# Latent queries' rotation: the identity product is dropped, and VectorE adds the turned rows to the part held in memory

## The chip, the cores and the metric

The kernel runs on one core of one Trainium2 chip. The metric is the device time of one execution in microseconds, from the first instruction to the last; lower is better. In each view PE is TensorE's matmuls, PEld its weight loads, DVE is VectorE, ACT is ScalarE, POOL is GpSimd.

## The reference, cut to what matters

The program is two models one after the other: a first block (dilated attention, a linear recurrence, two feed-forward parts) and then a second block of two equal layers. Each layer of the second block has three kinds of attention, one of them the "latent" one, which the change touches. It has 4 heads, 64 plain and 32 rotated dimensions per head, and a sequence of 512:

```
q = (rms_norm(c_q) @ w_uq)              # 512 x 4 heads x 96
k = concat(k_nope, k_r)                 # 64 own rows, 32 rows common to the heads
q = rms_norm(q, q_g);  k = rms_norm(k, k_g)
q = concat(q[:64], rope(q[64:], pos))   # the same for k
rope(x): concat(x1*cos - x2*sin, x2*cos + x1*sin)
p = softmax(mask(q @ k.T * 96**-0.5));  o = p @ v
```

So a rotated query is the query times a table of cosines, plus the query with its two halves exchanged (one with its sign turned) times a table of sines. Everything else in the program is unchanged and is left out here.

## The kernel before, in words

Activations lie transposed: features in the 128 partitions, the 512 tokens in the free dimension. Float32 products are made of three products of a high and a low part (`three`, L753 to L759). The high part is written by ScalarE, the low part by VectorE. Every engine has a program of its own, and they meet only at semaphores; the order on each engine is the order in which it is written.

Of a layer of the second block, the latent attention is the part named `mla_...`. A head (index h) goes through these steps:

- `mla_products(h)` on PE makes the head's raw query (96 rows) and raw key (64 rows) in two PSUM banks. Two banks are all that this part has for such outputs, so every use waits until VectorE has counted the bank of two uses ago as read (`acc_freed`).
- ScalarE squares both (`mla_squares`, L2244). VectorE's `mla_evict` writes the gained query times the cosine table to `turned` (L3130, a slice of the tile `sd`; in the 64 plain rows the table holds ones), the gained query times the sine table to `vt2` (L3132), and the gained key to `tn` (L3136).
- PE's `mla_sums` (L1396 to L1410) sums the key's squares over the rows (L1400) and then fills a second bank with the rotated query: an identity product that brings in `turned` (L1407) and a product with the constant `TURN`, which exchanges the halves of the 32 rotated rows of `vt2` and has zeros elsewhere (L1408). These are float32 products of 96x96 by 96x512, and the trace has two records for each.
- ScalarE's `mla_hi` makes the key's factor (L2254, L2258). VectorE's `mla_lo` multiplies the key by it (L3142) and then the rotated query in PSUM by its own factor `rs` (L3145). ScalarE copies both as high parts (L2261, L2267), VectorE writes both low parts (L2889).
- PE's `mla_scores(h)` (L1421 to L1424) makes four blocks of scores in four "wide" banks, with the sum for the next head's query factor (L1166) in front of the fourth. VectorE takes four maxima (L3168), ScalarE four exponentials (L2291), VectorE a reciprocal (L3176) and four scalings (L3180).
- PE's `mla_turn` transposes the weights into the wide banks (L785, L787), ScalarE copies them (L2058), VectorE takes the low parts (L2914) and so frees the wide banks for the next head's scores. `mla_weigh` applies them to the values.

The loop over the heads is written out. For head h, PE's order is: products of h+1, scores of h, weighing of h-1, sums of h+1, turning of h. VectorE's order is: `mla_evict` of h+1, maxima, output of h-1, reciprocal and scalings, `mla_lo` of h+1, low parts of the turned weights. So VectorE's `mla_lo` of the next head stands between the scalings of this head and the low parts that free the wide banks. Head 0's `mla_sums` and `mla_lo` stand ahead of the loop; behind `mla_lo(0)` ScalarE squares an output (L2023), PE sums the squares (L1166), ScalarE makes a factor of the sum (L2031), and PE turns a tile of values (L785, L787) in the same bank. Ahead of that sum PE runs ten matmuls whose result nobody reads (`unread_wide`, L778).

`mla_sums` runs 8 times in all: four heads in each of two layers.

Of the kernel before, what the change touches and what calls it, by code (L numbers as in the profile page):

```python
# [22 lines left out]
ALU = mybir.AluOpType  # L23
# [4 lines left out]
S = 512  # L28
# [30 lines left out]
MLA_W = 96  # L59
# [178 lines left out]
IDENT, ONES, HALVES, TURN, LATER, MINUS, FORBID = range(7)  # L238
# [27 lines left out]
def build_program(nc, t, out):  # L266

    with ExitStack() as ctx:
# [12 lines left out]
        sems = {n: ctx.enter_context(nc.semaphore(n)) for n in names}  # L281

        def sb(name, shape, dt=F32, c=ctx):
            return c.enter_context(nc.sbuf_tensor("s_" + name, shape, dt))

        bank = [ctx.enter_context(nc.psum_tensor(f"acc{n}", [P, S], F32)) for n in range(3)]
# [14 lines left out]
        square = sb("square", [P, FORBID + 1, P])  # L301
# [108 lines left out]
        tn = sb("tn", [P, 2, S], F32, stage)  # L410
        rs = sb("rs", [P, S], F32, stage)
# [11 lines left out]
        vt2, kr = (sb(n, [P, S], F32, sub) for n in ("vt2", "kr"))  # L423
        sd = sb("sd", [P, 2, TRI[TT]], F32, sub)
# [310 lines left out]
        def _(pe):  # L735
            count = Counts(pe)
            mm = nc.tensor.matmul
# [61 lines left out]
            for n, (a, b) in enumerate([(0, S), (S, 2 * S), (2 * S, F_W)]):  # L799
                o = wide[n // 2][0:GROUPS * HEADS, (n % 2) * S:(n % 2) * S + b - a]  # L800
# [319 lines left out]
            def layer(i):  # L1120
# [273 lines left out]
                def mla_sums():  # L1394


                    pe.wait_ge(sems["mla_sq"], count("mla_sq"))
                    if past := count("acc_freed", lag=count.banks):
                        pe.wait_ge(sems["acc_freed"], past)
                    mm(bank[count.bank()][0:MLA_W, :], square[0:MLA_W, ONES, 0:MLA_W], sq[0:MLA_W, 1, :], start=True,  # L1400
                       stop=True).then_inc(sems["acc_full"], 1)
                    count("acc_full")
                    count.outs += 1
                    if past := count("acc_freed", lag=count.banks):
                        pe.wait_ge(sems["acc_freed"], past)
                    o = bank[count.bank()][0:MLA_W, :]
                    mm(o, square[0:MLA_W, IDENT, 0:MLA_W], sd[0:MLA_W, 1, 0:S], start=True, stop=False)  # L1407
                    mm(o, square[0:MLA_W, TURN, 0:MLA_W], vt2[0:MLA_W, :], start=False, stop=True).then_inc(sems["acc_full"], 1)  # L1408
                    count("acc_full")
                    count.outs += 1  # L1410

# [36 lines left out]
                mla_values()  # L1448
                query_sum()
                mla_sums()  # L1450
                count("hn_lo")
                unread_wide(10, ckh)
# [3 lines left out]
                for h in range(HEADS_2):  # L1456
                    if h < HEADS_2 - 1:
                        mla_products(h + 1)
                    mla_scores(h)
                    if h == HEADS_2 - 1:  # L1460
                        head_sum(HALVES)
                    if h:
                        mla_weigh(h - 1, TT)
                    if h < HEADS_2 - 1:
                        mla_sums()
                    mla_turn()
# [86 lines left out]
                def mem_bank():  # L1553
                    if past := count("acc_freed", lag=count.banks):
                        pe.wait_ge(sems["acc_freed"], past)
                    o = bank[count.bank()]
                    count.outs += 1
                    return o
# [10 lines left out]
                for u in range(2):  # L1569
                    if u:  # L1570
                        pe.wait_ge(sems["unit_ready"], count("unit_ready"))
                    for n in range(0 if u else 2, 4):
                        o = mem_bank()
# [844 lines left out]
        def _(dve):  # L2418
            count = Counts(dve)
            count.squares = 0  # L2420
            tt, stt, ts = nc.vector.tensor_tensor, nc.vector.scalar_tensor_tensor, nc.vector.tensor_scalar

            def output():
                dve.wait_ge(sems["acc_full"], count("acc_full"))
                o = acc[count.bank()]
                count.outs += 1
                return o
# [447 lines left out]
            def layer(i):  # L2875
# [11 lines left out]
                def head_lo(dst, src, hi, scale=1.0):  # L2887
                    dve.wait_ge(sems["hn_hi"], count("hn_hi"))
                    stt(dst, src, scale, hi.bitcast(F32), ALU.mult, ALU.subtract).then_inc(sems["hn_lo"], 1)  # L2889
                    dve.wait_ge(sems["hn_lo"], count("hn_lo"))  # L2890
# [231 lines left out]
                R, KR = slice(0, MLA_W), slice(SUB, MLA_W)  # L3122
                turned, rs_k = sd[:, 1, 0:S], sd[:, 1, S:2 * S]
# [15 lines left out]
                def mla_lo(h):  # L3139
                    dve.wait_ge(sems["hn_rstd"], count("hn_rstd", 2))  # L3140
                    output()
                    tt(kr[R, :], tn[R, 1, :], rs_k[R, :], ALU.mult).then_inc(sems["acc_freed"], 1)  # L3142
                    dve.wait_ge(sems["acc_freed"], count("acc_freed"))
                    o = output()
                    tt(tn[R, 0, :], o[R, :], rs[R, :], ALU.mult).then_inc(sems["acc_freed"], 1)  # L3145
                    dve.wait_ge(sems["acc_freed"], count("acc_freed"))
                    head_lo(mla_k[h % 2][1], kr[R, :], mla_k[h % 2][0])
                    head_lo(mla_q[h % 2][1], tn[R, 0, :], mla_q[h % 2][0], MLA_W ** -0.5)
# [10 lines left out]
                mla_evict()  # L3159
                mla_values()  # L3160
                mla_lo(0)
                head_norm([(yo[:, 5, :], od[:], 0)], "sb_out_g_2")
                memory_values_lo()
                for h in range(HEADS_2):
                    if h < HEADS_2 - 1:
                        mla_evict()
                    for q in range(TT):
                        nc.vector.tensor_reduce(sm[:, q:q + 1], next_wide()[:, 0:(q + 1) * P], AX_X, ALU.max,  # L3168
                                                negate=True).then_inc(sems["nmax_ready"], 1)
                        count("nmax_ready")  # L3170
                    if h == HEADS_2 - 1:
                        mla_norm(0)
                    if h:
                        take_output(slice(SUB * ((h - 1) % 2), SUB * ((h - 1) % 2 + 1)))
                    dve.wait_ge(sems["exp_done"], count("exp_done", TT))
                    nc.vector.reciprocal(sm[:, 16:20], sm[:, 8:12]).then_inc(sems["recip"], 1)  # L3176
                    dve.wait_ge(sems["recip"], count("recip"))
                    for q in range(TT):
                        w = slice(TRI[q], TRI[q + 1])
                        ts(sd[:, 0, w], sd[:, 0, w], sm[:, 16 + q:17 + q], None, ALU.mult).then_inc(sems["wide_freed"], 1)  # L3180
                        count("wide_freed")
                    if h < HEADS_2 - 1:
                        mla_lo(h + 1)
                    else:
                        ys(range(3))
                    for q in range(TT):
                        turned_a(q)
# [60 lines left out]
                for n in range(2):  # L3248
                    o = output()
# [87 lines left out]
```

## Time and profile before

| | us |
|---|---|
| median of 3 runs | 3185.25 |
| lowest and highest | 3183.9, 3186.6 |
| the profiled execution's own time | 3184.36 |
| its span in the trace | 3182.5 |
| mean granted clock of TensorE | 0.988 of full |

A row of a timeline gives the start, the duration, the engine, the line, the operation with its tiles, and in square brackets how long the engine had been idle and what released it. Where a row says "x2", two records stand in it. Weight loads have rows of their own (PEld). Time in which an engine waited for nothing that the profile shows is called "issue".

### The profile page before, as it was taken

What the parts mean: (1) busy time and instruction counts of PE and PEld (TensorE: products, weight loads), DVE (VectorE), ACT (ScalarE), POOL (GpSimd) and SP (SyncE); (2) the same over time, 40 slices, a digit from 0 to 9 for tenths busy, and PEclk for the clock granted to TensorE, in tenths of its full rate; (3) what the DMA queues carried; (4) which work ended last, traced back from release to release, by engine and by line L of the source; (5) the groups of instructions that cost most, each with busy time, mean ns of one, the idle gap of its engine ahead of it and who ended that gap; (6) DMA issues with size and microseconds to landing.
All of it is one profiled execution on the core that took longest, in us unless ns stands there. A gap on an engine that the chain in (4) does not pass through costs nothing.

```text
span 3182.5 us, 44000 instructions
## 1 busy us (share of the span) xinstructions
PE 3071.7 (97%) x13735; PEld 2433.7 (76%) x13735; DVE 1632.5 (51%) x2425; ACT 1444.4 (45%) x2116; POOL 737.1 (23%) x508
## 2 busy tenths in 40 slices
PE   8999999999999999999999889999999988999998
PEld 6888888788887777888867667788887775778887
DVE  6544455585565878575668464511125746441113
ACT  4333334453334775342356764522245666552224
POOL 2333323100000000000022213244443220334444
PEclk9999999999999999999999999999999999999999
DMA  5333322333332232433312112133332210223334
GB/s 159 106 98 87 93 75 78 90 117 102 97 92 86 67 106 80 139 94 93 86 54 61 58 37 67 47 97 95 92 119 67 60 56 27 67 70 96 93 92 132
DMA packets 490394, 273.00 MB, mean 86 GB/s; under 512 B 9550, under 2 KB 479766, under 8 KB 489848
## 3 DMA queue, kind: packets, MB, share of 16 engines
q1 hardware_dynamic: 485576, 264.45, 28.9%
q10 hardware_dynamic: 4656, 6.58, 0.6%
q8 instruction: 78, 1.28, 0.2%
q14 instruction: 84, 0.69, 0.1%
HBM read 267.69 MB, written 12.21 MB: 88 GB/s over the span
## 4 chain that ended last, share of the span: by engine, by line
issue 56%; PE 30%; POOL 11%; DVE 2%; ACT 1%; POOLq 0%; ACTq 0%; DMA 0%; DVEq 0%
PE acc L753 9%; PE acc L754 9%; PE acc L759 8%; POOL s_w_lo L722 5%; POOL s_w_lo L721 5%; PE acc L756 1%; PE wide L785 1%; PE misc L754 0%; PE misc L753 0%; PE misc L759 0%; DVE s_sc L2610 0%; PE wide L753 0%; POOLq L111 0%; PE wide L754 0%; PE misc L785 0%
## 5 line engine op out<-in xcount | busy, mean ns | idle before, releaser
L753 PE MATMUL acc<-s_h_hi,s_w_hi 128*128 128x512 f32 (+1 forms) x1920 | 787.6, 410 | 15.0 <-DVE s_h_lo L3049 8.3
L754 PE MATMUL acc<-s_h_lo,s_w_hi 128*128 128x512 f32 (+1 forms) x1920 | 754.0, 393 | 0.0
L721 POOL TENSOR_TENSOR s_w_lo<-s_raw,s_w_hi 128x512 fp32r<-128x512 f32 x212 | 275.7, 1300 | 2035.3 <-ACT s_w_hi L1622 2034.0
L759 PE MATMUL acc<-s_h_hi,s_w_lo 128*128 128x512 f32 (+1 forms) x1680 | 660.5, 393 | 0.0
L1622 ACT ACTIVATE s_w_hi<-s_raw 128x1024 fp32r<-128x1024 f32 x386 | 409.6, 1061 | 367.6 <-DVE s_x L3298 211.3
L753 PEld LDWEIGHTS acc<-s_h_hi,s_w_hi 128*128 128x128 f32 x1920 | 363.8, 189 | 113.1 <-issue 16.9
L754 PEld LDWEIGHTS acc<-s_h_lo,s_w_hi 128*128 128x128 f32 x1920 | 364.5, 190 | 86.4 <-issue 11.3
L759 PEld LDWEIGHTS acc<-s_h_hi,s_w_lo 128*128 128x128 f32 x1680 | 318.6, 190 | 73.3
L704 POOL TENSOR_TENSOR s_w_lo<-s_raw,s_w_hi 128x1024 fp32r<-128x1024 f32 x80 | 191.6, 2395 | 403.3 <-ACT s_w_hi L1622 401.7
L722 POOL TENSOR_TENSOR s_w_lo<-s_raw,s_w_hi 128x512 fp32r<-128x512 f32 x212 | 278.6, 1314 | 0.0
L753 PE MATMUL acc<-s_hid_hi,s_w_hi 128*128 128x512 f32 x704 | 278.1, 395 | 0.0
L754 PE MATMUL acc<-s_hid_lo,s_w_hi 128*128 128x512 f32 x704 | 277.9, 395 | 0.0
L759 PE MATMUL acc<-s_hid_hi,s_w_lo 128*128 128x512 f32 x616 | 243.2, 395 | 0.0
L3288 DVE SCALAR_TENSOR_TENSOR s_u<-acc,s_rstd 128x512 f32<-128x512 f32 x64 | 44.3, 692 | 267.6 <-PE acc L756 260.1
L753 PE MATMUL wide<-s_h_hi,s_w_hi_f 128*128 128x512 f32 x384 | 153.4, 399 | 3.2 <-DVE s_h_lo L2444 3.2
L754 PEld LDWEIGHTS acc<-s_hid_lo,s_w_hi 128*128 128x128 f32 x704 | 132.4, 188 | 31.4
L753 PEld LDWEIGHTS acc<-s_hid_hi,s_w_hi 128*128 128x128 f32 x704 | 132.4, 188 | 31.4
L1840 ACT ACTIVATE s_cv<-s_up,s_cols 128x512 f32<-128x512 f32 x96 | 78.6, 819 | 162.0 <-DVE s_up L2690 157.7
L754 PE MATMUL wide<-s_h_lo,s_w_hi_f 128*128 128x512 f32 x384 | 151.7, 395 | 0.0
L2698 DVE SCALAR_TENSOR_TENSOR s_cv<-s_up,s_cols,s_cv 128x512 f32<-128x512 f32 x192 | 144.1, 750 | 6.1
L3298 DVE TENSOR_TENSOR s_x<-s_x,acc 128x512 f32<-128x512 f32 x48 | 33.0, 688 | 222.0 <-PE acc L756 222.0
L759 PEld LDWEIGHTS acc<-s_hid_hi,s_w_lo 128*128 128x128 f32 x616 | 115.9, 188 | 27.7
(498 smaller groups left out, 5414.9 us busy)
## 6 DMA issues: line engine op xcount, KB each, us to landing
s_raw<-w_ff SPq DMA_DIRECT2D x128, 512.0 KB, 4.0
s_raw<-ffn_w_up SPq DMA_DIRECT2D x96, 512.0 KB, 3.9
s_raw<-attn_w_qkv SPq DMA_DIRECT2D x72, 512.0 KB, 3.8
s_raw<-ffn_w_down SPq DMA_DIRECT2D x48, 512.0 KB, 3.9
s_raw<-w_in SPq DMA_DIRECT2D x48, 512.0 KB, 4.0
s_raw<-lru_w_in SPq DMA_DIRECT2D x16, 512.0 KB, 3.9
s_raw<-w_out SPq DMA_DIRECT2D x16, 512.0 KB, 4.0
s_bd<-bias_by_head SPq DMA_DIRECT2D x24, 256.0 KB, 5.0
```

Source lines behind the costliest of these rows:

```text
L704: pool.tensor_tensor(w_lo_of[w][:], raw[s][:], w_hi_of[w][:].bitcast(F32), ALU.subtract).then_inc(sems["unit_ready"], 1)
L721: pool.tensor_tensor(w_lo_b[s][:, 0:h, :], raw_b[s][:, 0:h, :], w_hi_b[s][:, 0:h, :].bitcast(F32), ALU.subtract)
L722: pool.tensor_tensor(w_lo_b[s][:, h:, :], raw_b[s][:, h:, :], w_hi_b[s][:, h:, :].bitcast(F32), ALU.subtract).then_inc(sems["unit_ready"], 1)
L753: mm(out, ahi, bhi, start=start, stop=False, **kw)
L754: mm(out, ahi, blo, start=False, stop=False, **kw)
L756: mm(out, alo, bhi, start=False, stop=stop, **kw).then_inc(sems[sem], 1)
L759: mm(out, alo, bhi, start=False, stop=stop, **kw)
L1622: fn(dst[:], src[:], ACT.Copy).then_inc(sems["hi_split"], 1)
L1840: fn(cv[:, s, :], up[:, s, 2:2 + S], ACT.Identity, bias=cols[:, bass.ds(b * KC + v, 1)], scale=cols[:, bass.ds(b * KC + w, 1)]).then_inc(s ...
L2698: stt(cv[:, s, :], up[:, s, tap:tap + S], cols[:, bass.ds(b * KC + w, 1)], cv[:, s, :], ALU.mult, ALU.add).then_inc(sems[sem], 1)
L3288: stt(u2[:, n % 2, :], o[:], 0.0, rstd[:], ALU.max, ALU.mult).then_inc(sems["acc_freed"], 1)
L3298: tt(x[:, n, :], x[:, n, :], o[:], ALU.add).then_inc(sems["acc_freed"], 1)
```

## The change

`mla_sums` no longer makes the identity product. The product with `TURN` starts and ends its bank's sum by itself, and the bank then holds only the turned rows. In `mla_lo` VectorE first adds the 32 rotated rows of that bank (`KR`, partitions 64 to 95) onto `turned` in place, waits for its own result, and multiplies `turned` instead of the bank by `rs`. The bank is counted as read by the multiplication, as before.

```diff
@@ mla_sums, TensorE
-                    o = bank[count.bank()][0:MLA_W, :]
-                    mm(o, square[0:MLA_W, IDENT, 0:MLA_W], sd[0:MLA_W, 1, 0:S], start=True, stop=False)
-                    mm(o, square[0:MLA_W, TURN, 0:MLA_W], vt2[0:MLA_W, :], start=False, stop=True).then_inc(sems["acc_full"], 1)
+                    mm(bank[count.bank()][0:MLA_W, :], square[0:MLA_W, TURN, 0:MLA_W], vt2[0:MLA_W, :], start=True,
+                       stop=True).then_inc(sems["acc_full"], 1)
@@ mla_lo, VectorE
                     o = output()
-                    tt(tn[R, 0, :], o[R, :], rs[R, :], ALU.mult).then_inc(sems["acc_freed"], 1)
+                    tt(turned[KR, :], o[KR, :], turned[KR, :], ALU.add).then_inc(sems["a_mid"], 1)
+                    dve.wait_ge(sems["a_mid"], count("a_mid"))
+                    tt(tn[R, 0, :], turned[R, :], rs[R, :], ALU.mult).then_inc(sems["acc_freed"], 1)
                     dve.wait_ge(sems["acc_freed"], count("acc_freed"))
```

## Rows read from the trace of the kernel before

**Rows 1.** Page, part 1: busy us (share of the span) and instructions.
```profile
PE 3071.7 (97%) x13735; PEld 2433.7 (76%) x13735; DVE 1632.5 (51%) x2425; ACT 1444.4 (45%) x2116; POOL 737.1 (23%) x508
```

**Rows 2.** Timeline of the first layer, PE's sums for heads 0 and 1.
```profile
1858.12 1.10 PE L1407 MATMUL acc<-s_sd,s_square 96*96 96x512 f32 x2
...
1871.98 1.02 PE L1407 MATMUL acc<-s_sd,s_square 96*96 96x512 f32 x2
...
1872.83 1.02 PE L1408 MATMUL acc<-s_vt,s_square 96*96 96x512 f32 x2
```

**Rows 3.** The line of the identity product, both layers.
```profile
L1407 PE MATMUL acc<-s_sd,s_square x16: 592/592/670, 1858.1 to 2677.6; 96*96 96x512 f32 x16
```

**Rows 4.** Timeline of the first layer, around head 0's query and what follows it.
```profile
1859.85 0.69 DVE L3142 TENSOR_TENSOR s_kr<-s_tn,s_sd 96x512 f32<-96x512 f32 x1
...
1860.66 0.69 DVE L3145 TENSOR_TENSOR s_tn<-acc,s_rs 96x512 f32<-96x512 f32 x1
1861.38 0.63 ACT L2267 ACTIVATE s_h_hi<-s_tn 96x512 fp32r<-96x512 f32 x1 [0.18 <-DVE s_tn L3145]
...
1862.12 0.63 ACT L2023 ACTIVATE s_sq<-s_od 128x512 f32<-128x512 f32 x1
...
1862.88 1.12 PE L1166 MATMUL misc<-s_sq,s_square 128*128 128x512 f32 x2 [0.51 <-ACT s_sq L2023]
...
1864.86 0.55 PE L785 MATMUL misc<-s_square,s_cq 128*128 128x128 f32 x3 [0.86 <-ACT s_rs L2031]
```

**Rows 5.** The lines of two other VectorE operations on 32 partitions, both layers.
```profile
L3090 DVE TENSOR_TENSOR s_cq<-misc,s_rope x2: 689/689/689, 1832.7 to 2611.6; 32x512 f32<-32x512 f32 x2
...
L3094 DVE TENSOR_TENSOR s_tn<-s_tn,s_cq x2: 1661/1662/1664, 1834.1 to 2613.3; 32x512 f32<-32x512 f32 x2
```

**Rows 6.** Timeline of the first layer, from head 0's scalings to head 1's scores.
```profile
1874.77 0.18 DVE L3176 RECIPROCAL s_sm<-s_sm 128x4 f32<-128x4 f32 x1 [2.75 <-ACT s_sd L2291]
...
1875.32 0.33 PE L787 MATMUL wide<-s_square,s_sd 128*128 128x128 f32 x1 [1.47 <-DVE s_sd L3180]
...
1879.66 1.74 DVE L2914 TENSOR_TENSOR s_al<-wide,s_ah 128x128 fp32r<-128x128 f32 x4 [0.21 <-DVE s_h_lo L2889]
...
1880.36 0.22 PE L1421 MATMUL wide<-s_h_hi 96*128 96x128 f32 x1
```

**Rows 7.** Timeline of the first layer, the same places for heads 2 and 3.
```profile
1888.23 0.14 PEld L787 LDWEIGHTS wide<-s_square,s_sd 128*128 128x128 f32 x1 [0.42 <-DVE s_sd L3180]
...
1892.57 0.62 DVE L2914 TENSOR_TENSOR s_al<-wide,s_ah 128x128 fp32r<-128x128 f32 x2 [0.21 <-DVE s_h_lo L2889]
...
1892.92 0.33 PE L1421 MATMUL wide<-s_h_hi 96*128 96x128 f32 x1 [0.62 <-DVE s_al L2914]
...
1905.58 0.33 PE L1421 MATMUL wide<-s_h_hi 96*128 96x128 f32 x1 [3.04 <-DVE s_al L2914]
```

**Rows 8.** PE's waits over the whole span: us in total, times, longest us.
```profile
PE wide L1421 <- DVE s_al L2914: 7.3, 4, 3.0
...
PE wide L787 <- DVE s_sd L3180: 5.7, 4, 1.5
```

**Rows 9.** Windows of 2 us, first layer: length, busy (x) of PE, PEld, DVE, ACT, POOL, PEclk, DMA.
```profile
1862.00:1864.00 2.00, 1.49 (x4) 0.30 (x2) 0.85 (x2) 0.64 (x2) 0.00 (x0) 1.00 0.00 0
1864.00:1866.00 2.00, 1.14 (x8) 0.99 (x8) 0.50 (x1) 1.74 (x3) 0.00 (x0) 1.00 0.00 0
...
1872.00:1874.00 2.00, 1.85 (x5) 0.47 (x3) 0.01 (x1) 1.67 (x7) 0.00 (x0) 1.00 0.00 0
1874.00:1876.00 2.00, 0.68 (x4) 0.43 (x5) 1.20 (x5) 1.86 (x4) 0.00 (x0) 0.96 0.01 4
1876.00:1878.00 2.00, 2.00 (x10) 1.85 (x10) 1.68 (x4) 0.98 (x3) 0.00 (x0) 0.50 0.00 0
1878.00:1880.00 2.00, 2.00 (x8) 1.29 (x7) 1.66 (x4) 1.63 (x4) 0.00 (x0) 0.69 0.00 0
```

**Rows 10.** Timeline of POOL: its first instruction after the last at 1854.90.
```profile
1931.80 1.29 POOL L721 TENSOR_TENSOR s_w_lo<-s_raw,s_w_hi 128x512 fp32r<-128x512 f32 x1 [75.61 <-ACT s_w_hi L1622]
```

## The prediction

> **What bounds the kernel now.** I read the page's first part first: PE is busy 97% of the span and VectorE 51% [rows 1]. A change that takes work from PE and gives it to VectorE looks like a gain by that. But the share is a mean over the program, and the change touches only the latent attention of two layers, some 70 us each (in the first layer from 1858 [rows 2] to 1932 [rows 10]). So I read the timeline of that stretch next, and then PE's waits. PE does not set the pace there: it waits for the low parts of the turned weights before a head's scores, 7.3 us in four waits, and for the scaled weights before their transposes, 5.7 us in four waits [rows 8]. The first layer alone shows 0.62 and 3.04 us before the scores of heads 2 and 3 [rows 7], so 3.66 of the 7.3, and the second layer repeats it. The reader is to see a ring of dependences there: scores, maxima, exponentials, reciprocal, scalings, the next head's key and query on VectorE, low parts of the turned weights, next scores. Each step waits for the one before, on another engine or on VectorE itself.
>
> **What is removed: the identity product.** Its two records start at 1871.98 and the TURN product starts at 1872.83, so it holds PE for 0.85 us [rows 2]. There are 16 records, that is 8 products [rows 3]: 6.8 us of PE's time. What is it worth? In head 1's sums PE is done with both products at about 1873.85 (1872.83 + 1.02, [rows 2]) and then idles 1.47 us until the first scaled weights are there at 1875.32 [rows 6]; ending 0.85 earlier makes that idle time 2.32 and moves nothing. For heads 2 and 3 the gap on PE is nearly closed: the weight load shows 0.42 us [rows 7]. There the transposes can start up to a few tenths earlier, but what follows waits for the low parts from VectorE (0.62 and 3.04 us, [rows 7]), so this too is worth nothing. For head 0, PE waits 0.51 us for the squares behind the query [rows 4], and again the earlier end only lengthens the wait. VectorE's multiplication does not wait for the product either: in each of the eight instances L3145 starts 0.81 us after L3142, back to back (1859.85 and 1860.66, [rows 4]). Value of the removal: nothing, as long as PE is not the last. I bound it by 0 and 6.8 us and take 0.
>
> **What is added: one VectorE addition and a wait for it.** No row has this instruction. The nearest are the product of a 32x512 PSUM operand with a 32x512 tile, 0.689 us, and an addition of two 32x512 tiles in memory, 1.66 us [rows 5]. The duration on 96 partitions is the same as on 32, 0.69 us [rows 4], so the smaller number of rows buys nothing. The 1.66 us were taken while POOL worked; here POOL does nothing for 75.6 us ahead of 1931.8, that is from 1856.2 [rows 10]. I take 0.69 us, and with the wait for its own semaphore the spacing of two dependent VectorE instructions, 0.81 us [rows 4]. Behind the addition in VectorE's queue stand the multiplication, both low parts, and the low parts of the turned weights; ScalarE's copy of the query (L2267) waits for it, and PE's next scores wait for all of these. The multiplication reads memory in place of PSUM: L3142 does that, and takes the same 0.69 as L3145 [rows 4]; cost 0.
>
> The Trainium skill, "SBUF — State Buffer", section "Who interferes with whom", says that a VectorE instruction with two SBUF inputs contends with a GpSimd instruction that reads SBUF, and that the second to issue blocks until the first is done. The new multiplication has become such an instruction. By that rule each would cost up to about a microsecond more if POOL worked beside it; POOL is idle through the stretch, so the rule leaves the sum as it is.
>
> **The delay, instance by instance.**
> - Head 0: the query is 0.81 later, ScalarE's copy and squares follow it back to back (1861.38, 1862.12), PE's sum waits for them (0.51 us idle before), then ScalarE's factor, then PE's transposes (0.86 us idle) [rows 4], then the next products and scores on PE. No slack: 0.81.
> - Head 1: the low parts that free the banks start at 1879.66, and the scores of head 1 start at 1880.36 behind PE's own products [rows 6]. At head 2 the scores start 0.35 after the first low part (1892.57 and 1892.92, [rows 7]), so head 1's scores could have started at 1880.01: slack 0.35, delay 0.81 - 0.35 = about 0.45.
> - Heads 2 and 3: PE waits for the low parts directly [rows 7]: 0.81 each.
>
> That is 0.81 + 0.45 + 0.81 + 0.81 = 2.88 us in a layer, 5.8 us in two. Nothing after it gives this back: the next products need the outputs of this attention, and weights are already waiting (POOL had stopped because its buffers were full, [rows 10]).
>
> **TensorE's clock.** More idle time can also cost clock. In the first layer the granted clock stays at 1.00 through the two windows with 1.49 and 1.14 us of PE work around head 0's sum, and it falls to 0.50 (1.2 of 2.4 GHz) after the two windows with 1.85 and 0.68 us; it is back within the window from 1878 [rows 9]. The low stretch is (0.04 x 2 + 0.50 x 2 + 0.31 x 2) / 0.5 = 3.4 us long, and costs PE half of that, 1.7 us. Before, it fell on the products of head 2, which nobody was in need of: only the slack of 0.35 above was used by it. Now take head 0's place: the unread matmuls end 0.85 earlier, the sum starts 0.81 later, so the wait before it is 0.51 + 0.85 + 0.81 = 2.2 us, with 0.86 after it [rows 4]. Of the 2.63 us of work in the two windows some 0.8 move out, leaving 1.8, less than the 2.53 after which the clock fell [rows 9]. So I expect it to fall here too. What comes next is transposes, products and scores on PE with everyone waiting, so the stretch is on the path: 1.7 us a layer at most, and 1.5 taken, since the transposes at its head are spaced by more than the clock. For two layers 3.0 us.
>
> The Trainium skill, "TensorE: Matmul & The Clock Gate", section "HAM oscillation — how this bites in real kernels", states it as a mechanism: idle gaps between bursts of matmuls put the clock back to half, and the next burst starts cold. The rule speaks against this change, which turns PE work into PE idle time, and the row of the low stretch bears it out; without the rule and the fall the sum would end at 5.8 us.
>
> **The sum.** 5.8 + 3.0 = 8.8 us. On the profiled execution's own 3184.36 (a span of 3182.5) that is 3193.2. Its time lies 0.9 below the median of the runs, 3185.25, so for a median I give 3194.1.
>
> **The rivals.**
> - Delay alone (A2): the clock does not fall at head 0, or in one layer only. 5.8 us give 3191.1, with one fall 3192.6. For it: the clock stood before with waits of 0.51 and 0.86 us. Against: the wait is now 2.2.
> - More clock is lost (A3): the wait before head 2's scores grows from 0.62 to 1.4 us, and the low stretch at head 3 grows or begins earlier; one more fall of 1.7 in each layer gives 3194.1 + 3.4 = 3197.5. Against: before 1892.9 PE has worked nearly without pause.
> - PE is the last after all (B), the other side: the 0.85 us of PE counts in each head, and the addition is hidden beside it. 3185.25 - 6.8 = 3178.4. It would need PE's sums to end later than the scaled weights are ready. Heads 2 and 3 are nearly at that point (0.42 us on the weight load, [rows 7]). It decides if the waits before L1421 are shorter than they seem; the 3.66 us a layer speak against it.
> - The delay is absorbed (C): some of it falls into slack that I don't see, as at head 1, so that less than 5 us remain: 3185.25 to 3190.
> - VectorE is slowed by POOL (D): the addition and the multiplication take 1.66 each, 8 x 2 x 0.97 = 15.5 us more: 3209.6. POOL would have to work in the stretch, and it doesn't [rows 10].
>
> **How the numbers follow.** Forecast 0.45; A2 0.30; A3 0.13; B 0.04; C 0.07; D 0.01. The range reaches from the low end of A2 (5.8 less 1 for a partly hidden instance, 3190.0) to A3's full price, 3198.0, and leaves out B, C, D and the edges of the others. 0.2% is 6.4 us, about what a measurement of this kernel can tell from no change; that is 3191.6. Slower by over that: the forecast, A3, D, and the part of A2 with one fall, 0.13, together 0.72. Within: the rest of A2 and C, 0.24. Faster: B, 0.04.
>
> **What would show it.** In the profile after, PE's busy time is lower and the kernel slower. The addition is a row of 0.69 us with the multiplication 0.81 after it; the wait before head 0's L1166 is about 2.2, before L787 of head 0 about 2.3, before L1421 about 1.4 for head 2 and 3.9 for head 3, and head 1 has a wait of some tenths where it had none. PEclk falls to 0.50 right after head 0's sum. Wrong would be: no growth of the waits before L1421 (B or C), an addition clearly longer or shorter than 0.69, or a clock that stays at 1.00 in head 0's place (then A2).

## The result, and the profile after

The changed kernel takes 3198.54 us (median of 6 runs, 3195.97 to 3201.09), the kernel before 3186.26 us beside it (6 runs, 3183.9 to 3187.34). The ratio is 1.0040, with a 95% interval of 1.0029 to 1.0051: 12.3 us slower, where 8.8 were forecast. The direction came as forecast, and so did the delay and the fall of the clock at head 0; two further costs of the clock did not, and the time lies 0.5 us above the range.

The page of the profile after, its first lines (the span is that of one profiled execution, whose own time is 3199.52):

```profile
span 3197.7 us, 43984 instructions
...
PE 3075.1 (96%) x13719; PEld 2435.8 (76%) x13719; DVE 1637.7 (51%) x2433; ACT 1443.1 (45%) x2116; POOL 736.6 (23%) x508
```

PE has 16 records fewer and VectorE 8 instructions more, which is the change. But PE's busy time is 3.4 us longer than in [rows 1], not 6.8 us shorter: the matmuls that are left took longer, which is a first sign of the clock. This is the timeline of the first layer after, the places of [rows 4, 6, 7] (start, length, engine and line, and in brackets the idle time before and what ended it):

```profile
1862.96 0.69 DVE L3141 TENSOR_TENSOR s_kr<-s_tn,s_sd 96x512 f32<-96x512 f32 x1
1863.77 0.69 DVE L3144 TENSOR_TENSOR s_sd<-acc,s_sd 32x512 f32<-32x512 f32 x1
1864.49 0.69 DVE L3146 TENSOR_TENSOR s_tn<-s_sd,s_rs 96x512 f32<-96x512 f32 x1
1865.21 0.63 ACT L2266 ACTIVATE s_h_hi<-s_tn 96x512 fp32r<-96x512 f32 x1 [0.90 <-DVE s_tn L3146]
...
1866.71 1.12 PE L1166 MATMUL misc<-s_sq,s_square 128*128 128x512 f32 x2 [2.08 <-ACT s_sq L2022]
...
1880.70 0.33 PE L787 MATMUL wide<-s_square,s_sd 128*128 128x128 f32 x1 [2.32 <-DVE s_sd L3181]
...
1899.50 0.33 PE L1420 MATMUL wide<-s_h_hi 96*128 96x128 f32 x1 [1.22 <-DVE s_al L2913]
...
1913.01 0.48 PE L1420 MATMUL wide<-s_h_hi 96*128 96x128 f32 x1 [3.76 <-DVE s_al L2913]
```

The addition (L3144) takes 0.69 us and starts 0.81 after the key's multiplication, but the query's multiplication follows it by 0.72, not 0.81. So the query comes 0.72 later. The waits are close to those that were named: 2.08 us before head 0's sum (2.2 named), 2.32 before the transposes behind head 0's scores (2.3), 1.22 before head 2's scores (1.4), 3.76 before head 3's (3.9). The wait of some tenths at head 1 did not come. In the last row the matmul itself takes 0.48 us, where [rows 7] has 0.33: it runs at a lower clock. In the waits over the whole span, these two lines answer to [rows 8] (us in total, times, longest):

```profile
PE wide L787 <- DVE s_sd L3181: 10.4, 8, 2.3
PE wide L1420 <- DVE s_al L2913: 10.0, 4, 3.8
```

The windows around head 0's sum, of after (length, busy (x) of PE, PEld, DVE, ACT, POOL, granted clock, DMA share, GB/s), where the first two of [rows 9] show 1.00:

```profile
1867.00:1869.00 2.00, 1.15 (x4) 0.32 (x4) 0.00 (x0) 1.02 (x2) 0.00 (x0) 0.91 0.00 0
1869.00:1871.00 2.00, 2.00 (x8) 1.56 (x7) 1.28 (x2) 0.90 (x2) 0.00 (x0) 0.50 0.00 0
```

The clock falls to its lower level (1.2 GHz) right behind head 0's sum, as forecast, and PE is fully busy while it is low, so this stretch is paid for.

**Where the 12.3 us are.** I cut both traces at the same instructions: the sine product of head 0 (L3132, after L3131), its key product, the first score matmul of each head, head 3's reciprocal, the first addition to the stream x. Each cell is the time from one to the next:

| us | key product | scores 0 | scores 1 | scores 2 | scores 3 | reciprocal 3 | addition to x | stage |
|---|---|---|---|---|---|---|---|---|
| before, layer 1 | 3.60 | 7.59 | 12.92 | 12.56 | 12.66 | 9.83 | 16.85 | 76.01 |
| after, layer 1 | 3.58 | 9.86 | 13.29 | 13.39 | 13.51 | 10.51 | 16.85 | 80.99 |
| before, layer 2 | 3.59 | 7.60 | 13.04 | 12.57 | 12.68 | 9.81 | 16.87 | 76.16 |
| after, layer 2 | 3.59 | 9.89 | 13.30 | 13.37 | 13.50 | 10.44 | 16.85 | 80.94 |

The stages cost 4.98 and 4.78 us more, together 9.8. The stretch from layer 1's addition to x to layer 2's sine product, in which no line was changed, is 2.3 us longer. It goes by the start times of these pairs; before:

```profile
1932.26 1.38 DVE L3197 TENSOR_TENSOR s_x<-s_x,acc 128x512 f32<-128x512 f32 x2 [1.05 <-PE acc L756]
...
2633.91 0.75 DVE L3132 SCALAR_TENSOR_TENSOR s_vt<-acc,s_cols,s_rope 96x512 f32<-96x512 f32 x1
```

after:

```profile
1940.37 0.69 DVE L3198 TENSOR_TENSOR s_x<-s_x,acc 128x512 f32<-128x512 f32 x1 [1.05 <-PE acc L756]
...
2644.34 0.75 DVE L3131 SCALAR_TENSOR_TENSOR s_vt<-acc,s_cols,s_rope 96x512 f32<-96x512 f32 x1
```

That is 701.65 before and 703.97 after. Behind layer 2's stage the two traces are equal (472.47 and 472.46 to the end). The three parts make 9.8 + 2.3 + 0 = 12.1 of the 12.3 measured. The two profiled executions differ by more, 15.2 us. The other 3.1 lie ahead of layer 1's stage, where nothing was changed: after is 3.9 us behind at 150 us, and 3.1 at the stage. At 150 us the other ten traces lie between 0.5 us ahead of before and 3.2 behind it, whatever their edit, so I take this for scatter between executions and leave it out.

### The profile page after: what moved, and what is told of

Read it like the earlier page. It is cut to its first block, busy times and chain, and to the rows that moved or that the text cites. A ratio compares the mean times of both kernels' runs of the same rounds, so it can differ in the third digit from the quotient of the medians.

```text
span 3197.7 us, 43984 instructions
## 1 busy us (share of the span) xinstructions
PE 3075.1 (96%) x13719; PEld 2435.8 (76%) x13719; DVE 1637.7 (51%) x2433; ACT 1443.1 (45%) x2116; POOL 736.6 (23%) x508
## 4 chain that ended last, share of the span: by engine, by line
issue 56%; PE 30%; POOL 11%; DVE 2%; ACT 1%; POOLq 0%; ACTq 0%; DMA 0%; DVEq 0%
PE acc L753 9%; PE acc L754 9%; PE acc L759 8%; POOL s_w_lo L722 5%; POOL s_w_lo L721 5%; PE acc L756 1%; PE wide L785 1%; PE misc L754 0%; PE misc L753 0%; PE misc L759 0%; DVE s_sc L2609 0%; PE wide L753 0%; POOLq L111 0%; PE wide L754 0%; ACTq L1668 0%
```

## The experiments

In each, "stage" and "stretch" are those of the table above. Times are medians, with the ratio to the kernel before run beside them.

**The changed kernel again**, with the first three experiments, so that they can be compared on one chip.

> The changed kernel once more, for a second trace and more timed runs. The latent stage (from head 0's key sum L1400 to the last ys product that waits) grew by 4.98 us in the first layer and 4.78 in the second in the first trace, 9.8 in all, of a difference of 15.2 between the two profiled executions. Theory A (only the stage pays, the rest is where TensorE's clock happens to fall in each execution): this trace shows 9 to 11 us again in the two stages, about 3197 us in all, and another amount outside them. Theory B (the change also costs something outside the stage, about 2.5 to 5 us): the first 1800 us are again 3.8 us longer and the stretch between the two latent stages again 2.3 us longer than in the trace of before.

3196.61 against 3185.16 us, ratio 1.0034 (1.0022 to 1.0047). The trace repeats the first to a few hundredths: stages 81.01 and 80.97, stretch 704.03. The falls of the clock are at the same places of the program in both layers, so they are no accident of one execution. The cost outside the stages is there again too (704.03 - 701.65 = 2.4 us), as the second theory had it.

**The removal alone.** The identity product and the addition both go, so this kernel leaves out the cosine part of every latent query; the query's factor is applied to the PSUM bank, as before:

```diff
-tt(turned[KR, :], o[KR, :], turned[KR, :], ALU.add).then_inc(sems["a_mid"], 1)
-dve.wait_ge(sems["a_mid"], count("a_mid"))
-tt(tn[R, 0, :], turned[R, :], rs[R, :], ALU.mult).then_inc(sems["acc_freed"], 1)
+tt(tn[R, 0, :], o[R, :], rs[R, :], ALU.mult).then_inc(sems["acc_freed"], 1)
```

> Half the change: the identity product is dropped and VectorE multiplies the bank as before, with no addition. It leaves out the cosine part of every latent query. Theory A (PE is not the last in this stage, so the product's 0.85 us are worth nothing, and more idle time can only cost clock): no faster than before, 3186.3, with the wait before head 0's sum 1.36 us in place of 0.51; if the clock falls there, up to 1.5 us a layer more, 3189.3. Rival B (PE's time is on the path, 8 x 0.85): 3179.5.

3186.79 against 3185.16 us, ratio 1.0003 (0.9994 to 1.0012). The stage of layer 1 is 76.01, that of before to the hundredth; that of layer 2 is 76.94, and what it has more comes in one step, from head 3's scores to its reciprocal (10.60 against 9.81), where its clock is low already when the scores begin. The product of 0.85 us, eight times, is worth nothing that can be measured.

**The addition alone.** The identity product is put back into its bank ahead of TURN, which overwrites it; VectorE keeps the addition:

```diff
-mm(bank[count.bank()][0:MLA_W, :], square[0:MLA_W, TURN, 0:MLA_W], vt2[0:MLA_W, :], start=True,
-   stop=True).then_inc(sems["acc_full"], 1)
+o = bank[count.bank()][0:MLA_W, :]
+mm(o, square[0:MLA_W, IDENT, 0:MLA_W], sd[0:MLA_W, 1, 0:S], start=True, stop=True)
+mm(o, square[0:MLA_W, TURN, 0:MLA_W], vt2[0:MLA_W, :], start=True, stop=True).then_inc(sems["acc_full"], 1)
```

> The other half: the changed kernel, with the identity product put back ahead of the TURN product in the same bank, where the latter overwrites it. PE has the work of before, VectorE the addition. Theory A (delay of 0.72 a head without slack, 0.4 at head 1): 2 x (3 x 0.72 + 0.4) = 5.1 us, 3191.4, if the clock stays at head 0 (wait of 0.51 + 0.72 = 1.2 us there), and 3194.4 if it falls. Rival: the whole of the change's cost comes from the addition and none from the work taken from PE: 3198.5.

3197.0 against 3185.16 us, ratio 1.0034 (1.0021 to 1.0048); stages 80.95 and 80.99, stretch 703.98. The whole cost of the change is the addition's. The two runs also test my reason for the fall of the clock at head 0: that too little of PE's work is left in the two windows of [rows 9]. Here are the wait before head 0's sum, the same two windows (from 5.75 us behind the start of the sine product) and the one behind them, first of the removal alone:

```profile
1864.72 1.12 PE L1166 MATMUL misc<-s_sq,s_square 128*128 128x512 f32 x2 [1.35 <-ACT s_sq L2022]
...
1863.86:1865.86 2.00, 1.12 (x2) 0.30 (x2) 0.83 (x2) 0.63 (x1) 0.00 (x0) 1.00 0.00 0
1865.86:1867.86 2.00, 1.16 (x7) 0.99 (x8) 0.52 (x1) 1.76 (x3) 0.00 (x0) 1.00 0.00 0
1867.86:1869.86 2.00, 2.00 (x13) 1.49 (x12) 1.37 (x3) 1.12 (x3) 0.00 (x0) 1.00 0.00 0
```

and of the addition alone:

```profile
1865.80 1.12 PE L1166 MATMUL misc<-s_sq,s_square 128*128 128x512 f32 x2 [1.20 <-ACT s_sq L2023]
...
1864.21:1866.21 2.00, 0.81 (x3) 0.30 (x2) 1.43 (x3) 1.26 (x2) 0.00 (x0) 1.00 0.00 0
1866.21:1868.21 2.00, 1.14 (x4) 0.44 (x3) 0.00 (x0) 1.14 (x2) 0.00 (x0) 0.85 0.00 0
1868.21:1870.21 2.00, 2.00 (x8) 1.55 (x7) 1.40 (x2) 0.77 (x2) 0.00 (x0) 0.50 0.00 0
```

The length of the one wait does not decide: with the longer wait, 1.35 us, the clock stands, and with the shorter, 1.20, it falls. PE's work in the two windows orders the kernels rightly. It is 2.63 us before and 2.28 in the removal alone, where the clock stands, and 1.95 in the addition alone and 1.56 after, where it falls. The removal takes its product away mostly ahead of these windows, while the delay of 0.72 us moves work out of them. But my yardstick, less than the 2.53 us at the other place, fails: 2.28 is less than that too, and the clock stands.

**More unread matmuls ahead of head 0's sum**, to keep PE at work and the clock up there. The kernel already has 10 that write a bank nobody reads:

```diff
-                unread_wide(10, ckh)
+                unread_wide(17, ckh)
```

> The changed kernel with 17 unread matmuls in place of 10 ahead of head 0's sum (7 x 0.23 = 1.6 us more of PE work in the wait of 2.1 us). Theory A (the clock that falls right after head 0's sum costs about 1.55 us a layer): the granted clock stays at full there and the kernel is 3.1 us faster than the changed one, 3195.4. Rival (the growth at head 0 from key product to scores, 2.27 us, is all delay, no clock): no difference, 3198.5.

3198.11 against 3185.16 us, ratio 1.0038 (1.0025 to 1.0052). The edit did what it was meant to do at its own place. Head 0's sum and the same windows:

```profile
1866.29 1.12 PE L1166 MATMUL misc<-s_sq,s_square 128*128 128x512 f32 x2 [0.52 <-ACT s_sq L2022]
...
1867.00:1869.00 2.00, 1.14 (x6) 0.67 (x6) 0.09 (x1) 1.33 (x3) 0.00 (x0) 1.00 0.00 0
1869.00:1871.00 2.00, 2.00 (x11) 1.38 (x10) 1.37 (x3) 1.18 (x2) 0.00 (x0) 1.00 0.00 0
```

The wait is 0.52 (0.51 in [rows 4]), PE's work in the two windows of [rows 9] is 2.62 us again, the clock stands, and from key product to scores it is 8.32 and 8.29 us instead of 9.86 and 9.89. That prices the fall at head 0 at 1.54 and 1.60 us a layer, 3.1 in all, and leaves the bare delay: 8.32 - 7.59 = 0.73, and 0.69. But the stage is 83.07 in layer 1 and 81.81 in layer 2, not shorter than after's: from head 2's scores to head 3's it now takes 15.93 and 15.90 us, where after takes 13.51 and 13.50. Windows from head 2's scores on:

```profile
1897.00:1899.00 2.00, 1.48 (x11) 1.41 (x12) 1.55 (x4) 1.68 (x3) 0.00 (x0) 0.99 0.02 4
1899.00:1901.00 2.00, 2.00 (x7) 1.47 (x6) 1.74 (x4) 0.59 (x1) 0.00 (x0) 0.50 0.00 0
1901.00:1903.00 2.00, 2.00 (x6) 1.21 (x4) 1.72 (x4) 0.71 (x2) 0.00 (x0) 0.50 0.00 0
...
1905.00:1907.00 2.00, 2.00 (x12) 1.73 (x11) 0.32 (x1) 1.41 (x4) 0.00 (x0) 0.81 0.00 0
```

A low stretch of some 6.8 us (three windows at 0.50, two of them shown, and 0.38 of the next) begins at head 2's scores, where after's clock stands at 1.00. One fall is gone and another, longer one has come. So the time is what the rival expected (3198.5, no difference), but the fall at head 0 did cost what the first theory said; it was paid elsewhere. In layer 1 head 3 costs more as well (11.02 from scores to reciprocal against 10.51, then 17.54 against 16.85), but the stretch behind is 701.40 again: the 2.3 us of after are not there. The two stages are 12.7 over before's with a stretch that costs nothing, and that comes to about as much as after's 9.8 + 2.3, by chance as far as these runs show.

**Two additions**: one more of the same kind, into a tile that nobody reads after it, ahead of the real one:

```diff
+tt(vt2[KR, :], o[KR, :], turned[KR, :], ALU.add).then_inc(sems["a_mid"], 1)
+dve.wait_ge(sems["a_mid"], count("a_mid"))
 tt(turned[KR, :], o[KR, :], turned[KR, :], ALU.add).then_inc(sems["a_mid"], 1)
```

> The changed kernel with a second addition of the same size in front of the first; its result goes to a slice that nobody reads before it is overwritten, and the addition waits for it. Theory A (the steps between the key product and the next scores are one chain with no slack left, so each addition costs its spacing of 0.72 us a head): the latent stage grows by 4 x 0.72 = 2.9 us a layer over the changed kernel, 5.8 in all, 3203.2 against 3197.4. Outside the stage theory A2 (the 2.35 us that the changed kernel loses ahead of the second layer's stage come from where TensorE's clock falls after a shift of the program by 5 us) expects another amount than 2.35, between 0 and 2.4, as the shift is now near 8 us; a rival in which the changed code itself costs those 2.35 us expects them again. Rival B (slack beside the chain, PE or ScalarE): under 0.5 us a head, 3201 or less.

3210.03 against 3184.94 us, ratio 1.0079 (1.0065 to 1.0093): 12.8 us over what the change costs. VectorE's own timeline shows what one addition costs there:

```profile
1859.87 0.69 DVE L3144 TENSOR_TENSOR s_vt<-acc,s_sd 32x512 f32<-32x512 f32 x1
1860.59 0.69 DVE L3146 TENSOR_TENSOR s_sd<-acc,s_sd 32x512 f32<-32x512 f32 x1
1861.32 0.69 DVE L3148 TENSOR_TENSOR s_tn<-s_sd,s_rs 96x512 f32<-96x512 f32 x1
```

0.72 us, and eight times that is 5.8, the forecast of theory A, which missed. The stages grew by 8.4 and 6.0, 14.4 in all, and the stretch fell back to 701.48, by 2.5; a rival in which the changed code itself costs those us expected them again. So a second equal delay costs about twice its own size, and part of it lies elsewhere than the first one's: head 0's 9.86 is now 11.21 in layer 1 and 10.61 in layer 2, and head 3's 13.51 is 17.85 and 16.51. The clock goes with it: its mean over the stages is 0.83 and 0.86, where after has 0.92 in both. This is not a sum of equal terms.

**ScalarE's order: the squares earlier**, in the kernel before. The squares for head 0's sum are made ahead of the key's and the query's high parts, and the unread matmuls go from 10 to 5:

```diff
-                mla_hi(0)
                 square_output()
+                mla_hi(0)
```

> The kernel before with one reordering at head 0 and nothing of the change: ScalarE squares the waiting output (L2023) ahead of head 0's high parts and not behind them, and PE's unread matmuls go from 10 to 5, so the sum over these squares no longer waits for the query. Theory A (the way from the query over the squares and the sum to the next products is what makes head 0 sensitive): the factor that follows (L2031) starts at the end of the query's high part, 1862.1 in place of 1864.1, 2.0 us a layer, 3181.2 against 3185.2 to 3186.3. Rival: another wait takes its place, no difference.

3185.2 against 3184.94 us, ratio 1.0000 (0.9991 to 1.0009). The stages are shorter by 1.64 and 1.77 (74.37 and 74.39); 0.8 of each is head 3's step to the reciprocal (9.02 us), where the low stretch of the clock is shorter. None of this shows in the median, though the interval leaves room for some 3 us either way. The start times of the stretch:

```profile
1932.63 1.39 DVE L3197 TENSOR_TENSOR s_x<-s_x,acc 128x512 f32<-128x512 f32 x2 [1.06 <-PE acc L756]
...
2636.47 0.75 DVE L3132 SCALAR_TENSOR_TENSOR s_vt<-acc,s_cols,s_rope 96x512 f32<-96x512 f32 x1
```

It is 703.84 us, as long as after's. The addition is not in this kernel, and layer 1's stage is shorter here, not longer. So the 2.3 us are no consequence of the addition as such. By the traces the stretch takes back 2.2 of the 3.4 us that the stages gain, and that is the larger part of why my expectation (4 us) missed.

**The addition off the chain.** This is the changed kernel in another order: squares early as above; the rotated query is made ahead of the key's sum; VectorE does the addition and the query's multiplication right behind its maxima, while it would wait for the exponentials; ScalarE makes the query's high part ahead of the key's, and VectorE takes the outputs of heads 0 and 1 behind the turned weights:

```diff
+                def mla_query():
+                    dve.wait_ge(sems["hn_rstd"], count("hn_rstd"))
+                    o = output()
+                    tt(turned[KR, :], o[KR, :], turned[KR, :], ALU.add).then_inc(sems["a_mid"], 1)
+                    dve.wait_ge(sems["a_mid"], count("a_mid"))
+                    tt(tn[R, 0, :], turned[R, :], rs[R, :], ALU.mult).then_inc(sems["acc_freed"], 1)
```

> The changed kernel with its addition moved off the chain: PE makes the rotated query first and the key's sum second, both ahead of the weighing of the head before; VectorE adds and multiplies right behind the maxima, where it waits for the exponentials anyway (0.9 to 2.7 us); the query's high and low part come ahead of the key's; and e5's order at head 0. Theory A (the addition costs only where it stands in the chain): the 4.98 and 4.78 us of the two stages are gone and some more with the multiplication, as fast as e7 within 2 us and faster than the kernel before, 3176 to 3182. Rival (an addition costs VectorE 0.72 us a head wherever it stands): 5 us slower than e7.

3183.1 against 3184.94 us, ratio 0.9996 (0.9987 to 1.0005). The stages are 75.48 and 73.16 us: what the change had added to them is gone, as theory A had it. Its times, 3176 to 3182 and within 2 us of the next kernel, were missed: this one is 4.0 us slower than the next, not far from the rival's 5. VectorE at head 1's query:

```profile
1884.42 0.69 DVE L3140 TENSOR_TENSOR s_sd<-acc,s_sd 32x512 f32<-32x512 f32 x1 [0.17 <-PE acc L1401]
1885.14 0.69 DVE L3142 TENSOR_TENSOR s_tn<-s_sd,s_rs 96x512 f32<-96x512 f32 x1
1887.01 0.18 DVE L3181 RECIPROCAL s_sm<-s_sm 128x4 f32<-128x4 f32 x1 [1.18 <-ACT s_sd L2289]
```

The same addition of 0.69 us stands in time that VectorE has to spare: 1.18 us of idle time is left before the reciprocal.

**The same order with the identity product.** The kernel before with this order, TURN accumulating on the identity product, and a multiplication alone in the new place.

> The same order as e6 on the kernel before: identity product kept, no addition, the query multiplied right behind the maxima. Theory A: the multiplication leaves the chain (0.8 us at heads 2 and 3, 0.3 at head 1, less some tenths since the copy of the output before now stands behind the turned weights), with e5's 2.0 us at head 0: 3 to 3.7 us a layer, 3178 to 3180.

3179.09 against 3184.94 us, ratio 0.9985 (0.9976 to 0.9994): 5.9 us below the kernel before, the fastest of all that were run. In layer 2 the steps from head 0's scores on are 11.75, 11.85, 12.42 us here and 11.75, 11.85, 12.70 with the addition, which thus costs some 0.3 us at one head, and 0.19 ahead of head 0's key product (5.31 and 5.12): half a microsecond a layer, not the rival's 0.72 a head. The rest of the 4.0 us between the two is in places where the clock differs: 12.99 against 11.74 us between the scores of heads 0 and 1 of layer 1, and from head 3's scores to its reciprocal 11.03 against 9.85 (9.82 against 9.15 in layer 2). Windows of layer 1, the addition off the chain, head 0's transposes and what follows:

```profile
1875.00:1877.00 2.00, 2.00 (x12) 1.49 (x12) 1.81 (x4) 1.69 (x3) 0.00 (x0) 0.77 0.00 0
1877.00:1879.00 2.00, 2.00 (x7) 1.15 (x6) 1.66 (x5) 1.66 (x4) 0.00 (x0) 0.50 0.00 0
```

and with the identity product:

```profile
1876.00:1878.00 2.00, 1.28 (x9) 0.95 (x10) 1.74 (x6) 1.75 (x5) 0.00 (x0) 1.00 0.00 0
1878.00:1880.00 2.00, 2.00 (x12) 1.41 (x11) 1.74 (x3) 1.62 (x4) 0.00 (x0) 1.00 0.00 0
```

**Is it the position?** Two kernels test it. In after and in before, some unread matmuls (8 in the one, 7 in the other) are added in the feed-forward part of the layers, far from the latent stage. The code of the stage is untouched, and all that comes behind them comes about 1.6 us later:

```diff
+                unread_wide(8, h_hi[:, 0, :])
```

> The changed kernel with 8 unread matmuls (8 x 0.233 = 1.86 us of pure PE work) in the feed-forward part of each layer, where PE is the bound and nothing of the change stands. Theory A2 (the 2.35 us that the changed kernel loses between the two latent stages come from where the shifted program meets the falls of TensorE's clock, not from its code): the stretch from the first layer's last output to the second layer's sine product, 701.65 us before and 703.97 in the changed kernel, is about 703.4, so 1.86 us of work cost -0.6 there; over both layers the kernel is 1.3 us slower than the changed one. Rival (the code of the change costs the 2.35): 705.8 in that stretch and 3.7 us slower than the changed kernel.

> The kernel before with 7 unread matmuls (7 x 0.233 = 1.63 us) at the same place, and nothing of the change. Theory A2: the shift of 1.63 us is about what the changed kernel's shift leaves over, so the same falls of the clock appear ahead of the second layer's latent stage: the stretch of 701.65 us grows to about 705.6, and the kernel is 5.6 us slower than before for 3.3 us of added work. Rival: 703.3 in that stretch, 3.3 us slower.

After with the shift: 3199.46 against 3186.91 us, ratio 1.0042 (1.0029 to 1.0056). Before with the shift: 3190.57 against 3186.91, ratio 1.0013 (1.0004 to 1.0022). That is 3.7 us slower, between 1.3 and 7.0, so the time alone can't tell the theory's 5.6 from the rival's 3.3; the traces can. The matmuls themselves cost 1.6 and 1.5 us, to be read behind layer 2's stage (474.08 and 473.96 against 472.46 and 472.47). The start times of the stretch, after with the shift:

```profile
1939.46 0.69 DVE L3199 TENSOR_TENSOR s_x<-s_x,acc 128x512 f32<-128x512 f32 x1 [1.06 <-PE acc L756]
...
2642.69 0.75 DVE L3132 SCALAR_TENSOR_TENSOR s_vt<-acc,s_cols,s_rope 96x512 f32<-96x512 f32 x1
```

before with the shift:

```profile
1933.17 1.38 DVE L3198 TENSOR_TENSOR s_x<-s_x,acc 128x512 f32<-128x512 f32 x2 [1.06 <-PE acc L756]
...
2638.80 0.75 DVE L3133 SCALAR_TENSOR_TENSOR s_vt<-acc,s_cols,s_rope 96x512 f32<-96x512 f32 x1
```

703.23 and 705.63 us. Less the matmuls' own cost, that is 701.6 for after and 704.1 for before: the two kernels have exchanged their stretches. The clock shows it. Windows of 10 us that begin 53 and 10 us ahead of layer 2's sine product, before and then before with the shift:

```profile
2580.91:2590.91 10.00, 5.38 (x20) 4.21 (x19) 3.81 (x6) 7.67 (x13) 0.79 (x2) 0.83 0.18 53
2623.91:2633.91 10.00, 7.41 (x47) 6.07 (x46) 4.38 (x5) 6.83 (x11) 7.81 (x7) 1.00 0.50 143
```

```profile
2585.80:2595.80 10.00, 7.18 (x26) 6.01 (x27) 3.99 (x6) 5.36 (x8) 2.54 (x2) 0.66 0.14 40
2628.80:2638.80 10.00, 7.43 (x35) 5.66 (x35) 3.64 (x5) 5.71 (x9) 7.50 (x6) 0.83 0.54 156
```

0.83 against 0.66 at the first place, 1.00 against 0.83 at the second: in each the clock is low for some 3.4 us more. After has the values of the shifted kernel before, and after with the shift those of before:

```profile
2591.34:2601.34 10.00, 7.09 (x26) 5.93 (x27) 4.08 (x6) 5.44 (x8) 2.52 (x2) 0.66 0.11 34
2634.34:2644.34 10.00, 7.46 (x35) 5.70 (x35) 3.62 (x4) 5.71 (x9) 7.46 (x6) 0.83 0.54 156
```

```profile
2589.69:2599.69 10.00, 5.41 (x20) 4.17 (x19) 3.81 (x6) 7.68 (x13) 0.81 (x2) 0.83 0.18 53
2632.69:2642.69 10.00, 7.43 (x47) 6.07 (x46) 4.40 (x5) 6.82 (x11) 7.90 (x7) 1.00 0.49 141
```

All twelve traces fall into these two groups, the added matmuls taken off. Seven have a stretch of 701.4 to 701.7 us and 0.83 and 1.00 in the windows (before, the removal alone, more unread matmuls, two additions, the addition off the chain, the same order with the identity product, after with the shift). Five have 703.8 to 704.1 us and 0.66 and 0.83 (both traces of after, the addition alone, the squares earlier, before with the shift). Neither the addition nor the removed product is what a group has in common. Each kernel but after has one trace only.

In the stage of layer 2 (81.81) the shift moves after's falls too: its steps are 8.31 (no fall at head 0), 13.29, 13.38, 15.90, those of the experiment with more unread matmuls. Where the clock falls thus depends on the time at which the program reaches a place, and matmuls added hundreds of microseconds earlier move it. Of the kernel before, the stage itself kept its time in both positions (75.95 and 76.00).

## Why the prediction was right or wrong

- **The removal, taken at 0: right.** The kernel without the product has before's stage of layer 1 to the hundredth, and its time within 0.1%. Rival B, PE as the last engine, is refuted by the same run.
- **The addition, 0.69 us: right. Its delay, 0.81: too much.** The spacing of two dependent VectorE instructions in [rows 4] was taken for every pair; the pair of addition and multiplication is 0.72 apart, in every trace looked at. Bare delays with the clock out of the way were 0.73 and 0.69 at head 0 (forecast 0.81), 0.37 and 0.26 at head 1 (0.45), 0.83 and 0.80 at head 2, 0.85 and 0.82 at head 3 (0.81 each): 5.4 us for the forecast 5.8. Heads 2 and 3 cost a tenth more than the 0.72, and the trace shows where: from a head's scores to the next key multiplication after takes 8.98 and 9.10 us, before 8.85 and 8.96. At head 2 VectorE's work behind the scores starts 0.36 us later against them, as head 1's slack is used up, and 0.13 of it arrives; at head 3 one low part of the turned weights waits 0.28 us for ScalarE's copy.
- **The clock at head 0, 3.0 us: right in size and place, its reason borne out in part.** It measured 3.1. I had argued that PE's work in the two windows falls to 1.8 us; it fell to 1.56. Over five kernels the two that fall are those with the least work there. That it falls because this is less than 2.53 was wrong: the removal alone has 2.28 and its clock stands. So the forecast of a fall had some luck in it, and what exactly decides stays open. The Trainium skill, "TensorE: Matmul & The Clock Gate", section "HAM oscillation — how this bites in real kernels", says that idle gaps between bursts of matmuls put the clock back; the gaps of its example are longer than the two compared here. This trace agrees that falls come with idle time, but not that the longer gap decides: 1.35 us cost nothing, 1.20 did.
- **The clock at head 3: named as rival A3, not in the sum.** Before, the fall began about 1 us into head 3's scores; the window of before:

```profile
1905.60:1907.60 2.00, 2.00 (x12) 2.00 (x13) 1.88 (x5) 1.64 (x4) 0.00 (x0) 0.74 0.01 4
```

  and of after, where it is low from their first matmul:

```profile
1913.00:1915.00 2.00, 1.99 (x10) 1.99 (x10) 1.67 (x4) 1.52 (x4) 0.00 (x0) 0.51 0.02 4
```

  This is the 0.68 and 0.63 us from head 3's scores to its reciprocal, 1.3 in all. The removal alone has the same step at 10.60 us in layer 2, without any addition, where its clock is low when the scores begin, and that bears the reading out.
- **The sum's missing terms: the step that failed.** The sum has the delay and one fall at head 0, and puts every other cost at nothing. I priced the change inside the stage alone, with no reason given for taking all code outside for unchanged in time as well. The program lost 2.3 us in the stretch between the layers, by falls of the clock at places that no line of the change touches. The shifts show that this is a matter of position. Inside the stage the sum left out head 3's 1.3 us, which stood as rival A3 alone.
- **The sum.** Forecast 5.8 + 3.0 = 8.8. By the traces 5.4 (delay) + 3.1 (head 0) + 1.3 (head 3) + 2.3 (stretch) = 12.1, against 12.3 measured (11.5 in the second measurement). The clock took 6.7 of it, more than the delay that set it off. The range had a bound for one more fall in each layer (3.4 us), and ended 0.5 below the time because nothing in it stood for the rest of the program.
- **Rivals C and D.** Nothing was absorbed beyond head 1's slack, and no addition took 1.66 us: all eight took 0.69.

```profile
L3144 DVE TENSOR_TENSOR s_sd<-acc,s_sd x8: 689/689/690, 1863.8 to 2694.4; 32x512 f32<-32x512 f32 x8
```

  (least, median and most in ns, first and last start). POOL's idle time, as read in [rows 10], held for both layers. That its buffers were full is not in that row: what ended the wait was ScalarE's next high part.
- **The signs.** PE's busy time was to be lower, and was 3.4 us higher: the 6.8 us of the product are gone, but at the low clock the matmuls that are left take more than that back.

## What to carry to other kernels

Ask of an edit on which chain its new instruction stands, not which engine has time on average: the same addition costs 0.72 us a head behind the scalings and some 0.5 a layer when it stands in VectorE's wait for the exponentials, while the 6.8 us of PE's work that it replaces are worth nothing where PE waits. And where the granted clock falls in short stretches, a small delay or a small gain has a second price, in either direction and also far from the edit: here 6.7 of 12.1 us, and by the traces 2.2 of the 3.4 us that the squares made early had gained. Before a difference of 0.1 to 0.2% is put down to an edit, run the kernel once more with a harmless shift ahead of it.

## What was not expected of the hardware

- A low stretch of the clock falls at the same instructions in two traces of the changed kernel, taken on different occasions, and moves when the program is shifted by 1.6 us.
- Removing one fall by giving PE more to do made another, longer one (6.8 us) two heads later.
- Which of two pauses costs clock can't be told from their lengths: one of 1.35 us cost nothing, one of 1.20 us in the same place, 0.72 us later, cost some 1.5 us in each layer.
- Dependent VectorE instructions of 0.69 us start 0.72 or 0.81 us apart: 0.81 behind the key's multiplication, 0.72 behind the addition. Neither the partitions nor an operand in PSUM makes the difference: L3130 and L3132 have 96 partitions and PSUM operands and start 0.78 apart at 0.75 each, so with the short gap too. What fits is the code between them, a wait for VectorE's own result alone in the short case, one for another engine besides in the long one; no run varied it.
